# The mixer's softmax probabilities: turned by TensorE, or by transposing transfers between a pack and a join

## What is computed

```python
scores = jnp.einsum('bnqhgd,bnshd->bhgnqs', qb, kb).astype(jnp.float32) * (HEAD_DIM ** -0.5)
...
scores = jnp.where(mask, scores, MASK_VALUE)
...
probs = jax.nn.softmax(jnp.concatenate([scores, sink], axis=-1), axis=-1)[..., :-1]
out = jnp.einsum('bhgnqs,bnshd->bnqhgd', probs.astype(v.dtype), vb)
```

## Time and profile before

| | |
|---|---|
| median of three runs | 1269.98 us |
| profiled execution | 1270.06 us |
| its span | 1268.0 us |
| TensorE busy | 1262.8 us |
| weight loads busy | 1070.7 us |
| VectorE busy | 916.8 us |
| ScalarE busy | 778.3 us |
| GpSimd busy | 84.1 us |
| queue of the weights | 62.1% of 16 DMA engines |

### The profile page before, as it was taken

How to read it: one execution, slowest core, us unless ns; L and a number is a source line. 1 busy time by engine, 2 the same in 40 slices (tenths; PEclk the granted TensorE clock), 3 DMA queues, 4 the chain that set the end, 5 groups by cost and what they waited for, 6 DMA issues and landing times.

```text
span 1268.0 us, 17729 instructions
## 1 busy us (share of the span) xinstructions
PE 1262.8 (100%) x7028; PEld 1070.7 (84%) x7028; DVE 916.8 (72%) x1050; ACT 778.3 (61%) x1014; POOL 84.1 (7%) x77
## 2 busy tenths in 40 slices
PE   9999999999999999999999999999999999999999
PEld 7888888987778888888888899888888889998887
DVE  6576556687987855556678787966867878798575
ACT  6676545568755666655676965554467687656441
POOL 0000000000000100000144000000012520000000
PEclk9999999999999999999999999999999999999999
DMA  9786737542466776663687767675658786657562
GB/s 349 235 289 228 220 102 251 174 122 83 150 229 209 242 232 203 210 229 125 170 240 191 228 206 208 185 226 177 208 170 248 193 221 219 202 157 226 181 199 83
DMA packets 144323, 254.33 MB, mean 201 GB/s; under 512 B 87024, under 2 KB 87152, under 8 KB 144112
## 3 DMA queue, kind: packets, MB, share of 16 engines
q1 hardware_dynamic: 141360, 244.35, 62.1%
q10 hardware_dynamic: 2880, 8.84, 2.2%
HBM read 232.19 MB, written 1.05 MB: 184 GB/s over the span
## 4 chain that ended last, share of the span: by engine, by line
PE 94%; DVE 3%; ACT 1%; issue 1%; DMA 1%; SPq 0%; POOL 0%; ACTq 0%; another core or an unknown queue 0%; DVEq 0%; POOLq 0%
PE psum L2097 24%; PE psum L2118 24%; PE psum L2098 24%; PE psum L2103 5%; PE psum L2150 5%; PE psum L2104 5%; PE psum L2296 2%; PE psum L2165 2%; PE psum L2550 1%; DVE w_lo L1308 1%; PE psum L2396 1%; DMA raw<-weights 1%; PE psum L2536 0%; PE psum L2313 0%; ACT w_hi L685 0%
## 5 line engine op out<-in xcount | busy, mean ns | idle before, releaser
L1308 DVE TENSOR_TENSOR w_lo<-raw,w_hi 128x1024 fp32r<-128x1024 f32 x219 | 265.6, 1222 | 139.6 <-ACT w_hi L685 138.3
L685 ACT ACTIVATE w_hi<-raw 128x1024 fp32r<-128x1024 f32 x219 | 228.8, 1055 | 121.9 <-PE psum L2118 74.1
L2097 PE MATMUL psum<-w_hi,x_hi 128*128 128x512 f32 x552 | 216.9, 393 | 0.0
L2098 PE MATMUL psum<-w_hi,x_lo 128*128 128x512 f32 x552 | 214.6, 389 | 0.0
L1308 DVE TENSOR_TENSOR y_lo<-raw,y_hi 128x1024 fp32r<-128x1024 f32 x139 | 168.8, 1221 | 51.6 <-ACT y_hi L685 50.8
L685 ACT ACTIVATE y_hi<-raw 128x1024 fp32r<-128x1024 f32 x139 | 145.9, 1055 | 60.3 <-PE psum L2118 24.5
L2118 PE MATMUL psum<-w_lo,x_hi 128*128 128x512 f32 x552 | 170.0, 389 | 0.0
L2097 PE MATMUL psum<-y_hi,x_hi 128*128 128x512 f32 (+1 forms) x376 | 147.5, 392 | 0.0
L2098 PE MATMUL psum<-y_hi,x_lo 128*128 128x512 f32 (+1 forms) x376 | 146.3, 389 | 0.0
L2097 PEld LDWEIGHTS psum<-w_hi,x_hi 128*128 128x128 f32 x552 | 103.8, 188 | 23.2 <-issue 2.0
L2118 PEld LDWEIGHTS psum<-w_lo,x_hi 128*128 128x128 f32 x552 | 103.7, 188 | 21.7 <-DVE w_lo L1308 0.4
(11 more groups left out here) (228 smaller groups left out, 2313.3 us busy)
## 6 DMA issues: line engine op xcount, KB each, us to landing
raw<-weights SPq DMA_DIRECT2D x406, 512.0 KB, 4.3
probs<-weights SPq DMA_DIRECT2D x8, 512.0 KB, 5.2
probs_t<-weights SPq DMA_DIRECT2D x8, 512.0 KB, 5.3
arena<-gains ACTq DMA_DIRECT2D x7, 512.0 KB, 4.5
arena<-gate_bias ACTq DMA_DIRECT2D x6, 512.0 KB, 4.5
norm<-x_feat SPq DMA_DIRECT2D x4, 256.0 KB, 5.1
res<-x SPq DMA_DIRECT2D x2, 512.0 KB, 8.4
arena<-lru_w ACTq DMA_DIRECT2D x1, 1024.0 KB, 4.7
```

The lines of the kernel that those rows point to most:

```text
L685: act.activation(slot(t)[0], raw_place(t), ACT.Copy).then_inc(hi_ready, 1)
L1308: dve.tensor_tensor(lo, raw_place(t), hi.bitcast(F32), ALU.subtract).then_inc(lo_ready, 1)
L2097: pe.matmul(out_, l_hi, r_hi, start=start, stop=False, skip_group_check=skip)
L2098: pe.matmul(out_, l_lo, r_hi, start=False, stop=False, skip_group_check=skip)
```

## The change

The transposes on TensorE and the copies out of PSUM are gone. In their place, for each unit, ScalarE packs the scaled probabilities into `planes` (for unit 0 at the end of chunk 6, for unit 1 between the two passes of the decay in chunk 7, for unit 2 ahead of both passes in chunk 8, for units 3 to 5 right behind their scaling), SP issues the transposing transfer ahead of the mixer's tiles 36, 40, 42, 46, 48 and 52, and VectorE joins the planes into `probs_t` in the next chunk, ahead of the mask of the next unit. `values1` moves from behind the first tile of the next chunk to behind the second, and reads `probs_t` with a stride, since the blocks are no longer put in another order. The scores of a unit wait for the previous unit's maximum instead of for the copies. The mask of a unit now waits for the previous pack. The six jobs of the mixer are counted ahead of those of the second block, so that block's numbers move by six; `planes_pack` itself is moved, unchanged.

```diff
-            return At(j + 1, l, 2 * DIL_GROUPS + UNITS_LAYER)
+            return At(len(UNITS1) + j + 1, l, 2 * DIL_GROUPS + UNITS_LAYER)
...
+        MIX_SWAP_AT = (36, 40, 42, 46, 48, 52)
+        PLANE_SWAPS.update({MIX_AT + at: u + 1 for u, at in enumerate(MIX_SWAP_AT)})
...
-            def probs_copy(u):
-                if u == 4:
-                    return
-                act.wait_ge(probs_turned, u)
-                act.activation(probs_t[:, 0:512], psum[:, 4, :], ACT.Copy).then_inc(probs_act, 1)
...
+            def planes_pack(job, words):
+
+                if job > 1:
+                    act.wait_ge(planes_joined, job - 1)
+                act.activation(by_plane(planes), by_word(words.bitcast(U16)), ACT.Copy).then_inc(planes_packed, 1)
+
+            def mix_pack(u):
+
+                if u < UNITS1_BY_DVE:
+                    act.wait_ge(probs_normed, u + 1)
+                else:
+                    act.wait_ge(probs_scaled, u - UNITS1_BY_DVE + 1)
+                planes_pack(u + 1, probs[:, :])
...
-                if 0 <= u - 1 < len(UNITS1):
-                    probs_copy(At(u))
...
                 if UNITS1_BY_DVE <= u < len(UNITS1):
                     scale_probs(u)
+                    mix_pack(u)
                 refill(t + 3)
+                if c == 6:
+                    mix_pack(u)
                 if c in (7, 8):
                     act.wait_ge(conv_done, 2)
+                    if c == 8:
+                        mix_pack(u)
                     decay_tanh(c - 7)
+                    if c == 7:
+                        mix_pack(u)
                     decay(c - 7)
...
+            def mix_join(u):
+
+                dve.wait_ge(planes_swapped, 16 * (u + 1))
+                if u:
+                    dve.wait_ge(values_ready, u)
+                dve.tensor_copy(by_word(probs_t.bitcast(U16)), by_plane(swapped)).then_inc(planes_joined, 1)
...
-                if 0 <= u - 1 < len(UNITS1) and c not in (11, 12):
-                    probs_copy(At(u), 8)
...
+                if 1 <= u <= len(UNITS1):
+                    mix_join(u - 1)
                 if 0 <= u < len(UNITS1):
...
+                    if u:
+                        dve.wait_ge(planes_packed, u)
                     mask_scores(At(u + 1), qt, n, mask_window)
...
-                if c in (10, 11):
-                    probs_copy(At(u + 1), 8)
...
-                probs_read(At(u + 1))
+                pe.wait_ge(planes_joined, u + 1)
...
+                turned = probs_t.rearrange("p (i j s n) -> p i s j n", i=2, s=qt + 1, n=P)
                 for s in range(qt + 1):
                     for i in range(2):
-                        first = (i * (qt + 1) + s) * n
-                        ins = pe.matmul(psum[i * HEAD:(i + 1) * HEAD, bank, at:at + n], v_cols(min(heads) + i, s),
-                                        probs_t[:, first:first + n], start=s == 0, stop=s == qt)
+                        out_ = psum[i * HEAD:(i + 1) * HEAD, bank, at:at + n].rearrange("p (j n) -> p j n", n=P)
+                        ins = pe.matmul(out_, v_cols(min(heads) + i, s), turned[:, i, s], start=s == 0, stop=s == qt)
...
-                        probs_read(At(u))
+                        pe.wait_ge(max_ready, At(u))
...
-                    if q == 0 and 1 <= u <= len(UNITS1):
+                    if q == 1 and 1 <= u <= len(UNITS1):
                         values1(u - 1)
-                if 0 <= u < len(UNITS1):
-                    by_dve = u < UNITS1_BY_DVE
-                    turn_probs(probs_normed if by_dve else probs_scaled, u + 1 if by_dve else u - UNITS1_BY_DVE + 1,
-                               places1(UNITS1[u][0]))
```

More of the change, by code:

```diff
@@ L401, in block_program @@
         DIL_SWAP_AT = (22, 32, 36, 40, 44, 48)
-        LAYER_SWAPS = {At(LAYER_AT, l, LAYER_TILES) + 52 + 15 * u // 4: unit_job(u, l)
+        PLANE_SWAPS = {At(LAYER_AT, l, LAYER_TILES) + 52 + 15 * u // 4: unit_job(u, l)
                        for l in range(LAYERS) for u in range(UNITS_LAYER)}
-        LAYER_SWAPS.update({At(LAYER_AT, l, LAYER_TILES) + at: dil_job(j, l)
+        PLANE_SWAPS.update({At(LAYER_AT, l, LAYER_TILES) + at: dil_job(j, l)
                             for l in range(LAYERS) for j, at in enumerate(DIL_SWAP_AT)})
+        MIX_SWAP_AT = (36, 40, 42, 46, 48, 52)
+        PLANE_SWAPS.update({MIX_AT + at: u + 1 for u, at in enumerate(MIX_SWAP_AT)})
         def by_word(v):
@@ L494, in block_program @@
         probs_scaled = sem("probs_scaled")
-        probs_turned = sem("probs_turned")
-        probs_act = sem("probs_act")
-        probs_dve = sem("probs_dve")
         planes_packed = sem("planes_packed")
@@ L593, in _ @@
                                            ).then_inc(hidden_swapped, 16)
-                if t in LAYER_SWAPS:
-                    sp.wait_ge(planes_packed, LAYER_SWAPS[t])
+                if t in PLANE_SWAPS:
+                    sp.wait_ge(planes_packed, PLANE_SWAPS[t])
                     sp.dma_start_transpose(swapped.rearrange("p (b s) -> p b s", s=P), planes[:, :]
@@ L1122, in dil_square @@
                     act.activation(probs[:, :], norm[:, (j + 1) % 2, :], ACT.Square).then_inc(dil_squares, 1)
[L1124 to L1128, removed]
                 def dil_pack(j):
@@ L2297, in scores @@
                 ins.then_inc(scores_ready, 1)
[L2299 to L2307, removed]
             def warm(n):
```

## The result

The changed kernel takes 1278.52 us (median of 4 runs, 1277.56 to 1278.79) against 1270.24 us of the kernel before beside it (1269.39 to 1270.93): ratio 1.0064, 95% interval 1.0047 to 1.0082, some 8.3 us slower. Predicted were 1277.9 us and +7.8. The profiled execution took 1278.48 us, its span is 1276.6 us against 1268.0.

The account below looks back on a forecast made before the run. TensorE was read as busy 100%, but without slack against ScalarE's queue and VectorE's recurrence at some chunk starts. Delays from packs and joins, carried through the chunks, reached +7.8 us: 1270.06 + 7.8 = 1277.9, range 1273.5 to 1282.0.

Parts of the forecast that it names:

- Step 1: Chunk 6: pack 0 falls where ScalarE waited; chunk 7 starts 0.4 us sooner (bounds -0.5 and 0).
- Step 2: Chunk 7: pack 1 ahead of the second decay pass; the tanh that frees the banks +0.9 us, chunk 8 +0.75.
- Step 3: Chunk 8: pack 2 ahead of both decay passes; ScalarE's split of tile 105 +2.3 us, mask 2 +0.95.
- Step 4: Chunk 9: VectorE waits for that split, join 2 adds 1.25; mask 3 +3.5 us, values 2 wait from 315.8 to 316.9.
- Step 5: Chunks 9 and 10: pack 3 makes the square root +5.3 us, join 3 mask 4 +6.55; values 3 wait over 5.
- Step 6: Scan and L1320 follow mask 4 and give nothing back; chunk 11, bound to L1320, starts +6.55 us.
- Step 7: Chunk 11: VectorE saves a copy (-0.6 us) and gets join 4 (+1.25); mask 5 and chunk 12's start +7.2.
- Step 8: Chunk 12: pack 5, swap and join end at 366.4, values 5 begin 0.6 us late; sum +7.8.
- The one line: Mixer loop: pack, landing and join, 6.7 to 8.0 us, now stand between a unit's scaled probabilities and the next mask.
- Rival (a): TensorE keeps the pace, packs and joins fit into idle time: -5.6 us, 1264.5 us; chance 5%.
- Rival (b): ScalarE absorbs the packs of chunks 8 and 9, only VectorE's joins count: +2.4 us, 1272.4 us; chance 8%.
- Rival (c): Transposing transfers land after 5.8 to 7.8 us because weight transfers are under way: 1283 us; chance 9%.

Follow-up runs that it names:

- gains late: Changed kernel with the decay gains' load moved from chunk 9 to chunk 13: 1277.97 us; the same with packs of units 1 to 5 cut small: 1273.42 us.
- experiment 1: Changed kernel with the joins of units 1 to 5 cut to 128 of 2048 halves; waits, packs and transfers stay: 1274.52 us, ratio 1.0036.
- experiment 2: Changed kernel with the packs of units 1 to 5 cut to 128 of 2048 halves; waits, transfers and joins stay: 1279.17 us, ratio 1.0071.
- experiment 4: Changed kernel with packs and joins of units 1 to 5 both cut to 128 of 2048 halves, gains' load in chunk 13: 1270.11 us, ratio 1.0001.
- experiment 5: Kernel before, with seven of eight TensorE transposes of each unit left out and nothing added: 1269.78 us, ratio 0.9999.
- experiment 6: Changed kernel with each join of units 0 to 4 moved behind the next unit's mask and maximum in VectorE's queue: 1281.86 us, ratio 1.009.
- experiment 7: Changed kernel with the values put back behind the first product of the next chunk: 1286.25 us, ratio 1.0126.
- experiment 8: Changed kernel with the packs on GpSimd instead of ScalarE: 1278.13 us, ratio 1.0066.

## Why the prediction was right

The changed trace stands 0.6 us behind that of before already ahead of the first instruction that differs in the mixer (merged transposes at 163.6 against 163.0 us). At that point the traces of the experiments stand anywhere between 0.55 us ahead of before (packs on GpSimd) and 0.74 behind (gains late), so this looks like scatter from one execution to the next, and 0.6 is taken off here. In us, predicted and measured:

| Step | Predicted | Measured less 0.6 |
|---|---|---|
| 1, 2: ScalarE copy that frees the banks | +0.9 | +0.8 |
| 3: split of tile 105 | +2.3 | +2.2 |
| 4: mask 3 | +3.5 | +3.4 |
| 4: wait of values 2 | 1.1 | 1.04 |
| 5: square root | +5.3 | +5.3 |
| 5: mask 4 | +6.55 | +6.2 |
| 5: wait of values 3 | over 5 | 5.17 |
| 6: chunk 11 starts | +6.55 | +6.5 |
| 7: mask 5 | +7.2 | +6.8 |
| 8: wait of values 5 | 0.6 | 0.41 |
| end of the mixer | +7.8 | +7.25 |

- **Step 1** holds. The chunk's own gain of 0.4 us shows as mask 1 at 0.3 us ahead of its old place.
- **Steps 2 to 5** hold in order and size up to the square root, and experiments 1 to 4 show that packs and joins are the whole price: 4.7 and 3.6 us. Mask 4 is 0.4 us below the forecast. Before, VectorE's gating by the root began 0.44 us after the root had ended (323.88 + 1.92 = 325.80), in the changed kernel 0.09 us after it (329.81 + 1.91 = 331.72, then 331.81); the step carried the whole delay of the root over. The row of before:

```profile
326.24 1.23 DVE L1619 TENSOR_TENSOR arena<-arena 128x1024 f32<-128x1024 f32 x1 [1.22 <-issue]
```

- **The one line** of the prediction puts the swap's landing on the path, 6.7 to 8.0 us between the scaled probabilities and the next mask, and there it is wrong. Swaps 3, 4 and 5 landed 4.5, 3.9 and 3.8 us after their issue (at 327.57, 345.48 and 361.01), 2.6, 0.8 and 0.4 us ahead of their joins (334.68, 350.20, 365.19); no mask waited for one. The loop that binds is that of the numbered steps: mask, exponentials, then the pack in ScalarE's queue, behind it a split or the root that VectorE waits for, then the join in VectorE's queue, next mask.
- **Step 6** has the right number partly by chance. L1327 ends at 344.61 against 337.84 before, 6.2 us later once the 0.6 are off, and by the gate that the step names chunk 11 would have started at about +6.2. It starts at 345.04. What came last was TensorE itself, slowed behind its long wait (below); it cost 0.3 us there and nothing later, because VectorE sets the start of chunk 12.
- **Steps 7 and 8**: from mask 4 to mask 5 the delay grows by 0.65 us, as predicted, so mask 5 and the start of chunk 12 (360.19 against 352.81 before, +6.8 once the 0.6 are off; predicted +7.2) only carry the 0.4 of mask 4. The gate of chunk 12 is L1327 (1.52 us of waiting), as step 7 had it by way of the mask. The wait of values 5 is 0.2 us below the forecast.
- **The sum** is 0.55 us too high in the mixer, which is these 0.4 and 0.2, and the median difference (8.3) is 0.5 higher than the sum. Of the span's +8.6 us, 7.25 arise in the mixer, 0.6 ahead of it and 0.7 behind 389.50. That the totals agree to 0.5 us is therefore partly luck: what the mixer fell short by, other stretches made up. Part of the 0.7 may be the change's: one block of eight turned also loses 0.7 us there, and both-small 1.05. No run took this stretch apart; it stays open.
- **What was costed at nothing**: the strided operand of the values is free (eight matmuls of 128x256 take 1.08 us, as the same eight did before, at 313.04); SP's held weight transfers delay nothing that TensorE waits for (ScalarE's split at 367.92 waits 5.04 us for a tile, where the longest such wait in this stretch was 3.28 before); the landings were 3.7 to 4.5 us.

Rival (a), TensorE keeps its pace, falls with mask 3 and with experiment 5. Rival (b), ScalarE absorbs the packs, falls with experiment 1. Rival (c), late landings, did not happen in the changed kernel, but experiment 2 shows it was a real one: one swap of 10.2 us undid 4.5 us of gain.

No version here beats the kernel before, and none is pointed to: even without the cost of packs and joins the time is that of before (experiment 4), since most of what the transposes cost TensorE was not what this stretch waited for. Other places for the packs within ScalarE's queue were not tried.

## What to carry over

Price work taken off the busiest engine by whether that engine has slack against the others' queues in that stretch; here waits of 0.2 to 0.3 us with a releaser on another engine were the sign that it had none, and experiment 5 bore it out. Work put onto an in-order queue can cost its whole length at everything behind it, and where that leads back to itself once per chunk, the costs of successive chunks add up. When an experiment moves a transfer, ask what it will be issued beside.

## What the runs showed of the hardware

**The clock after a wait.** Windows of the changed kernel (columns as above), behind the wait of 5.17 us:

```profile
330.00:336.00 6.00, 0.89 (x4) 0.38 (x3) 4.19 (x5) 5.92 (x5) 0.00 (x0) 0.86 0.69 165
336.00:341.00 5.00, 4.95 (x15) 3.23 (x16) 4.90 (x8) 2.21 (x10) 0.00 (x0) 0.50 0.25 91
341.00:345.00 4.00, 4.00 (x18) 3.23 (x18) 3.86 (x7) 3.97 (x6) 0.00 (x0) 0.98 0.00 0
```

TensorE was busy 0.89 of 6 us, then got 0.50 of its clock, the 1.2 GHz level, for about 5 us, and the full 2.4 GHz after. The eight value matmuls took 1.98 instead of 1.08 us, and the tile behind them 4.33 us (337.96 to 342.29) against 2.75 for the next (to 345.04): 2.5 us in all. All but 0.3 us of that was hidden here. In experiments 6 and 7, where other waits don't cover it, such a loss is the likely part that the expectations lacked; no run took the clock's share alone. A wait on TensorE can cost more than its length, and the length of one wait does not say whether it will. The values behind equal waits in experiments 6 and 8:

```profile
340.85 1.98 PE L2340 MATMUL psum<-probs_t,arena 128*64 128x256 f32 x8 [3.58 <-DVE probs_t L1512]
...
331.58 1.08 PE L2351 MATMUL psum<-probs_t,arena 128*64 128x256 f32 x8 [3.58 <-DVE probs_t L1525]
```

**A transposing transfer** of 0.5 MB within SBUF lands after 3.7 to 4.5 us in the changed kernel's mixer, and in experiment 2 once after 10.2 us, issued 1 us behind a weight tile and 0.17 us ahead of the gains' load.

**GpSimd beside VectorE**: in experiment 8 five of six GpSimd copies made what VectorE started beside them 1.1 to 1.7 us longer; beside the sixth it started nothing.
